# A router between two stages of a one-core transformer kernel: logits, ranks and fillers changed

## What is computed

```
h     = rmsnorm(x, norm2[1])
probs = softmax(h @ router)                 # 8 experts for each of 512 tokens
top_p, top_i = top_k(probs, 2)
top_p = top_p / sum(top_p)
gates = sum(one_hot(top_i, 8) * top_p)      # token x expert
out   = sum over e of gates[:, e] * swiglu(h, w_gate[e], w_up[e], w_down[e])
```

## Time and profile before

| | |
|---|---|
| profiled execution | 2717.13 us |
| its span | 2715.3 us |
| mean granted clock of TensorE | 0.986 |
| TensorE busy | 2601.9 us, 96% |
| VectorE busy | 1575.6 us, 58% |
| ScalarE busy | 1189.9 us, 44% |
| router's stage | from about 1043.5 to 1070.3 us |
| experts' stage | from 1071.4 us |

### The profile page before, as it was taken

How to read it: one execution, slowest core, us unless ns; L and a number is a source line. 1 busy time by engine, 2 the same in 40 slices (tenths; PEclk the granted TensorE clock), 3 DMA queues, 4 the chain that set the end, 5 groups by cost and what they waited for, 6 DMA issues and landing times. The chain is left out here.

```text
span 2715.3 us, 54780 instructions
## 1 busy us (share of the span) xinstructions
PE 2601.9 (96%) x22741; PEld 2088.9 (77%) x22741; DVE 1575.6 (58%) x1974; ACT 1189.9 (44%) x1532; POOL 318.4 (12%) x360
## 2 busy tenths in 40 slices
PE   8999999999999988999999998999899999999998
PEld 7677678888777767788888887864778797788887
DVE  6747454244484755667676676377565545564462
ACT  5644343122355443555656564345334433432232
POOL 5123000000110401011111100021410000000002
PEclk9999899999999999999999999999999999999999
DMA  4200244334220022787787777412023342333341
GB/s 140 82 9 3 63 114 110 86 93 112 71 89 25 4 56 73 274 285 276 282 289 275 279 276 241 123 42 74 6 72 117 93 140 70 86 97 99 91 110 53
DMA packets 351884, 331.12 MB, mean 122 GB/s; under 512 B 17273, under 2 KB 269525, under 8 KB 351605
## 3 DMA queue, kind: packets, MB, share of 16 engines
q1 hardware_dynamic: 348101, 317.76, 37.6%
q0 software_dynamic: 3392, 11.14, 1.1%
q10 hardware_dynamic: 240, 0.07, 0.0%
HBM read 317.41 MB, written 11.53 MB: 121 GB/s over the span
## 5 line engine op out<-in xcount | busy, mean ns | idle before, releaser
L3234 DVE TENSOR_TENSOR experts_w_lo<-experts_raw,experts_w_hi 128x2048 fp32r<-128x2048 f32 (+1 forms) x81 | 167.6, 2079 | 76.2 <-ACT experts_w_hi L3190 74.9
L3234 DVE TENSOR_TENSOR experts_w_lo<-raw_in_act,experts_w_hi 128x2048 fp32r<-128x2048 f32 (+1 forms) x81 | 167.0, 2078 | 58.4 <-ACT experts_w_hi L3190 58.1
L3190 ACT ACTIVATE experts_w_hi<-raw_in_act 128x2048 fp32r<-128x2048 f32 (+1 forms) x81 | 139.7, 1746 | 49.1 <-DMA raw_in_act<-in_moe_up 43.6
L3403 PE MATMUL psum<-experts_w_hi,experts_xg_lo 128*128 128x512 f32 x384 | 155.0, 404 | 5.4 <-DVE experts_w_lo L3234 4.3
L1641 PE MATMUL psum<-keep_act_hi,proj_w_lo 128*128 128x512 f32 x360 | 151.0, 419 | 7.4 <-DVE proj_w_lo L1561 7.4
L3404 PE MATMUL psum<-experts_w_lo,experts_xg_hi 128*128 128x512 f32 x384 | 150.7, 392 | 0.0
L3405 PE MATMUL psum<-experts_w_hi,experts_xg_hi 128*128 128x512 f32 x384 | 150.6, 392 | 0.0
L3190 ACT ACTIVATE experts_w_hi<-experts_raw 128x2048 fp32r<-128x2048 f32 (+1 forms) x81 | 140.4, 1742 | 21.7 <-DMA experts_raw<-in_moe_gate 17.0
L1643 PE MATMUL psum<-keep_act_hi,proj_w_hi 128*128 128x512 f32 x360 | 140.5, 390 | 0.0
L1642 PE MATMUL psum<-keep_act_lo,proj_w_hi 128*128 128x512 f32 x360 | 140.3, 390 | 0.0
L862 PE MATMUL psum<-keep_act_hi,conv_ffn_w_lo 128*128 128x512 f32 x336 | 131.9, 392 | 2.3 <-DVE conv_ffn_hid_lo L913 2.3
(11 more groups left out here) (867 smaller groups left out, 6834.1 us busy)
## 6 DMA issues: line engine op xcount, KB each, us to landing
raw_in_act<-in_moe_gate SPq DMA_DIRECT2D x33, 1024.0 KB, 7.2
experts_raw<-in_moe_up SPq DMA_DIRECT2D x32, 1024.0 KB, 10.4
experts_raw<-in_moe_down SPq DMA_DIRECT2D x32, 768.0 KB, 11.6
raw_in_act<-in_moe_down SPq DMA_DIRECT2D x32, 768.0 KB, 6.8
conv_ffn_raw<-in_w_ffn_in SPq DMA_DIRECT2D x43, 512.0 KB, 5.0
experts_raw<-in_moe_gate SPq DMA_DIRECT2D x17, 1024.0 KB, 8.7
raw_in_act<-in_moe_up SPq DMA_DIRECT2D x16, 1024.0 KB, 5.2
proj_raw<-in_w_in SPq DMA_DIRECT2D x18, 768.0 KB, 4.4
```

The costliest lines, as they stand in the source:

```text
L3190: act.activation(w_hi[v % 2][:, s], raw[ring][:, 0:n], ACT.Copy).then_inc(rounded, 1)
L3234: dve.tensor_tensor(w_lo[v % 2][:, s], raw[ring_of(2 * v + q)][:, 0:n], w_hi[v % 2][:, s].bitcast(F32), ALU.subtract).then_inc(split, 1)
L3403: pe.matmul(out, lhs[1][:, first + k, :], w_hi[slot][:, cols], start=begin and k == 0, stop=False)
```

## The change

The logits are made with plain fp32 products, in token order at once: for each of the eight tiles and each token group, h is the loaded operand and the eight columns of the router's weights are streamed. With that the rounding and the rest of h and of the weights go, as do the copy by expert and its four transposes. Their buffers go too. The logits are compared unscaled, and only the argument of the exponential is multiplied by the root. The root itself is one square root on ScalarE, with its table asked for in advance by a dummy activation, and a reciprocal on VectorE. The sums of squares stand behind the logits and two turns of rows.

The comparisons of all four token groups are one instruction each (256 elements). The prefix sum reads PSUM; chosen is turned twice, and ScalarE copies the second for the later product. The number of tiles is one comparison against four limits and one sum. ScalarE also copies the nth table, which VectorE did. The eight pieces of rows are spread: two before the sums, three behind them, three behind the tile sum, with ScalarE's keeps in groups of 1, 3, 2 and 2. The turns of the identity become 0, 6 and 0 in the router in place of 10, 22 and 24, and 10 in place of 22 at the opening of the experts.

```diff
@@ class Route
     def aside(self, job):
         def scalar(act, j, group):
                     self.square(act, k)
-                    self.round(act, k)
         def vector(dve, j, group):
                     self.weigh(dve, k)
-            if group >= 2:
-                for k in (2 * group - 4, 2 * group - 3):
-                    self.rest(dve, k)
@@ scalar
-            act.wait_ge(m.early.landed, w_landed)
-            act.activation(w_hi[:, :, :], w, ACT.Copy).then_inc(parts, 1)
             for k in LATE:
-                route.round(act, k)
                 route.square(act, k)
+            act.activation(no_root[:, :], m.ones[:, 0:1], ACT.Sqrt)
             act.wait_ge(summed, 1)
-            act.activation(root_tok[:, :], ps[:, 0, 0:TT], ACT.Ln, scale=1.0 / D, bias=m.eps[:, 0:1]).then_inc(root, 1)
-            act.wait_ge(root, 1)
-            act.activation(root_tok[:, :], root_tok[:, :], ACT.Exp, scale=-0.5).then_inc(root, 1)
-            act.wait_ge(root, 2)
+            act.activation(length_tok[:, :], ps[:, 0, 0:TT], ACT.Sqrt, scale=1.0 / D, bias=m.eps[:, 0:1]).then_inc(root, 1)
+            act.wait_ge(v_done, STEPS["root"])
-            keep(range(0, 3))
-            act.wait_ge(centred, 1)
+            keep(range(0, 1))
+            act.wait_ge(centred, 3)
             act.activation(prob[:, :, :], prob[:, :, :], ACT.Exp).then_inc(exped, 1)
-            keep(range(3, 8))
+            keep(range(1, 4))
             act.wait_ge(t_full, 2)
+            act.activation(chosen_t[0:E, :], ps[0:E, 7, :], ACT.Copy).then_inc(chosen_kept, 1)
+            act.wait_ge(t_full, 3)
             act.wait_ge(filled, 5)
             act.activation(tall[PROB, :], ps[0:E, 1, :], ACT.Copy).then_inc(prob_kept, 1)
+            keep(range(4, 6))
+            act.wait_ge(nth_full, 1)
+            act.activation(tall[NTH, :], ps[0:E, 7, :], ACT.Copy).then_inc(nth_kept, 1)
+            keep(range(6, 8))
@@ tensor
-            turn_identity(m, pe, ps[:, 2, 0:P], 10)
-            pe.wait_ge(parts, 2)
+            pe.wait_ge(m.early.landed, w_landed)
             for k in range(DT):
-                ...
-            last.then_inc(full, 1)
+                pe.wait_ge(route.weighted, k + 1)
+                for t in range(TT):
+                    last = pe.matmul(ps[:, 7, t * E:(t + 1) * E], h[:, k, t * P:(t + 1) * P], w[:, k, :], ...)
+            last.then_inc(logits_full, 1)
+            for n in range(2):
+                turn(n)
             (the four products of the sums)
-            (the four transposes of the logits by expert)
-            for n in range(8):
+            for n in range(2, 5):
                 turn(n)
-            turn_identity(m, pe, ps[:, 1, 0:P], 22)
+            pe.wait_ge(root, 1)
+            turn_identity(m, pe, ps[:, 1, 0:P], 6)
             pe.wait_ge(v_done, STEPS["prob"])
-            for b, src in enumerate((chosen, prob)):
+            for b, src in ((0, chosen), (7, chosen), (1, prob)):
                 (four transposes each)
-            pe.wait_ge(v_done, STEPS["chosen_t"])
+            pe.wait_ge(chosen_kept, 1)
             (the product that counts chosen over experts)
             pe.wait_ge(v_done, STEPS["tiles"])
             (the product that sums the tiles)
+            for n in range(5, 8):
+                turn(n)
             pe.wait_ge(prob_kept, 1)
-            turn_identity(m, pe, ps[:, 1, 0:P], 24)
+            pe.wait_ge(nth_kept, 1)
@@ vector
+            step(dve.tensor_copy(logits[:, :, :], ps[:, 7, 0:TT * E].rearrange("p (t e) -> p t e", t=TT)))
+            dve.wait_ge(root, 1)
+            step(dve.reciprocal(root_tok[:, :], length_tok[:, :]))
+            dve.tensor_reduce(top[:, :], logits[:, :, :], AX.X, ALU.max).then_inc(centred, 1)
+            (prob = (logits - top) * root_tok in two instructions)
-            for t in range(TT):
-                (two comparisons of 128 x 64)
+            own = logits[:, :, :].unsqueeze(3).to_broadcast([P, TT, E, E])
+            other = logits[:, :, :].unsqueeze(2).to_broadcast([P, TT, E, E])
+            step(dve.tensor_tensor(above[:, :, :, :], other, own, ALU.is_gt))
+            step(dve.tensor_tensor(ties[:, :, :, :], other, own, ALU.is_equal))
             dve.wait_ge(t_full, 1)
-            step(dve.tensor_copy(chosen_t[0:E, :], ps[0:E, 0, :]))
-            step(dve.tensor_tensor_scan(run[0:E, :], ..., chosen_t[0:E, :], 0.0, ALU.mult, ALU.add))
-            (one step and three pairs of steps for the limits)
+            step(dve.tensor_tensor_scan(run[0:E, :], ..., ps[0:E, 0, :], 0.0, ALU.mult, ALU.add))
+            step(dve.tensor_scalar(more[0:E, :], limits[0:E, :], run[0:E, T - 1:T], None, ALU.is_lt))
+            step(dve.tensor_reduce(tiles[0:E, :], more[0:E, :], AX.X, ALU.add))
+            dve.wait_ge(chosen_kept, 1)
             step(dve.tensor_tensor(tall[RUN, :], run[0:E, :], chosen_t[0:E, :], ALU.mult))
-            dve.wait_ge(nth_full, 1)
-            step(dve.tensor_copy(tall[NTH, :], ps[0:E, 7, :]))
@@ experts_phase, tensor
-            turn_identity(m, pe, ps[:, 7, 0:P], 22)
+            turn_identity(m, pe, ps[:, 7, 0:P], 10)
             list_slots(0)
             turn_identity(m, pe, ps[:, 7, 0:P], 52)
```

More of the change, by code:

```diff
@@ L2720, in __init__ @@
         self.h = m.nc.alloc_sbuf_tensor_at("route_h", [P, DT, T], F32, offset=ROUTE_AT)
[L2721 to L2732, removed]
+        self.ring = m.nc.alloc_sbuf_tensor_at("route_sq", [P, 3, T], F32, offset=ROUTE_AT + DT * T * 4)
+        self.squared, self.added, self.weighted = (m.nc.alloc_semaphore(f"route_{n}") for n in ("squared", "added", "weighted"))
     def square(self, act, k):
@@ L2805, in route_phase @@
         tall, wide = ph.sb("tall", [P, T]), ph.sb("wide", [P, 3, N])
-        tiles, more, begin, end = (ph.sb(n, [P, 1]) for n in ("tiles", "more", "begin", "end"))
+        LIMITS = -(-T // SLOTS)
+        tiles, begin, end = (ph.sb(n, [P, 1]) for n in ("tiles", "begin", "end"))
+        limits, more = (ph.sb(n, [P, LIMITS]) for n in ("limits", "more"))
         mine, shift, before = (ph.sb(n, [P, N]) for n in ("mine", "shift", "before"))
@@ L2810, in route_phase @@
         ps = ph.banks()
[L2811 to L2815, removed]
+        consts, filled, summed, root, logits_full, centred, exped, turned, kept, stored = (
+            ph.sem(n) for n in ("consts", "filled", "summed", "root", "logits_full", "centred", "exped", "turned", "kept", "stored"))
+        v_done, t_full, chosen_kept, prob_kept, nth_full, nth_kept, ended, made = (
+            ph.sem(n) for n in ("v_done", "t_full", "chosen_kept", "prob_kept", "nth_full", "nth_kept", "ended", "made"))
         block = ph.enter_context(nc.Block())
@@ L2819, in route_phase @@
         LATE = range(route.EARLY, DT)
-        LIMITS = range(SLOTS, T, SLOTS)
         STEPS, n = {}, 0
-        for name, steps in (("prob", 11 + 2 + 2 * TT + 8), ("chosen_t", 1), ("tiles", 2 + 2 * len(LIMITS)), ("wide", 11)):
+        for name, steps in (("root", 12 + 2), ("prob", 2 + 4 + 4), ("tiles", 3), ("wide", 10)):
             n += steps
@@ L2886, in turn @@
                 last.then_inc(turned, 1)
[L2888 to L2889 removed]
+            pe.wait_ge(m.early.landed, w_landed)
             for k in range(DT):
[L2891 to L2894, removed]
[L2895 removed]
+                pe.wait_ge(route.weighted, k + 1)
+                for t in range(TT):
+                    last = pe.matmul(ps[:, 7, t * E:(t + 1) * E], h[:, k, t * P:(t + 1) * P], w[:, k, :], start=k == 0 and t == 0,
+                                     stop=k == DT - 1 and t == TT - 1, skip_group_check=True)
+            last.then_inc(logits_full, 1)
+            for n in range(2):
+                turn(n)
             pe.wait_ge(route.added, DT - 1)
@@ L2940, in _ @@
                 route.weigh(dve, k)
-            dve.wait_ge(parts, 1)
-            dve.tensor_tensor(w_lo[:, :, :], w, w_hi[:, :, :].bitcast(F32), ALU.subtract).then_inc(parts, 1)
-            for k in range(route.EARLY - 2, DT):
-                route.rest(dve, k)
             for k in LATE:
                 route.add(dve, k)
-            dve.wait_ge(full, 1)
-            dve.tensor_copy(by_expert[:, :], ps[0:E, 1, :]).then_inc(by_expert_done, 1)
             dve.wait_ge(consts, 5)
```

44 lines of the change are left out of this document (10 added, 34 removed).

## The result

| | before | after |
|---|---|---|
| median (runs), on one chip | 2719.03 us (4) | 2798.84 us (4), 2795.84 to 2803.45 |
| ratio after / before, 95% interval | | 1.0293 [1.0278, 1.0307] |
| profiled execution, its span | 2717.13, 2715.3 us | 2795.84, 2793.6 us |
| granted clock, mean | 0.986 | 0.970 |

The changed kernel is 2.9% slower. I had forecast 2715.2 us and a range up to 2722.6, so the forecast is wrong by ten times what a measurement can tell. The 78.3 us between the two spans, split at four points that both traces have.

The account below looks back on a forecast made before the run. It took TensorE, busy 96%, to be bound where it waits or fills time in the router's stretch. Gains of 3.7 (router) and 0.5 (experts' opening), 4.2 us, off a mean of 2719.4 gave 2715.2 us; range 2709.0 to 2722.6.

Parts of the forecast that it names:

- The step that failed: From the router to the code behind the gather: all of it moves by what the router saves, 4.2 us with the opening.
- five cases: The forecast of 2715.2 us (chance 0.45) and four rivals about router and experts' opening, all inside 0.3% (8.2 us).
- first rival: Router's logits: the clock falls after some 41 of 64 narrow records, net 0.5 us slower than before; chance 0.20.
- Logits and root: Router's head: 64 records take 7.4 us, reciprocal ready at 1053.3 where VectorE began at 1053.35; about nothing gained.
- Ranks: VectorE's comparisons in the router: two of 0.43 us in place of eight, first transpose at 1057.35 not 1058.48, 1.1 gained.
- Scan to placing products: Router after the ranks: scan from PSUM 1.25 us, tiles ready at 1059.75 not 1062.36, placing products from 1062.5 to 1063.7.
- The new last one: Router's end: SyncE's last store, after ScalarE's last kept rows, ends the stage at 1065.8 to 1067.3; 3.7 us gained.
- Opening: Start of the experts: 10 turns, not 22, at the low clock; 5.3 us against 5.8, 0.5 gained.
- Gather: Behind the experts' opening: the 52 turns take 5.87 us inside the gather's 7.4, so they don't show.
- third rival: Experts' opening: the 52 turns run at the low clock, 11.6 us, eating the whole gain, 2719.4 us; chance 0.05.

Follow-up runs that it names:

- pad22: The changed kernel with 22 empty TensorE instructions behind the router's last product: 2719.16 us, ratio 1.0012 to the kernel before.
- before_m44: The kernel before with 30 in place of 52 identity turns behind the first lists, 44 TensorE instructions less: 2794.85 us, ratio 1.0289.
- pad96: The changed kernel with 96 empty TensorE instructions behind the router's last product: 2769.24 us in one run.

## Why the prediction was wrong

**The step that failed** stood at the end of its first part: "what the router saves moves the gather, and everything behind the gather, by the same amount". Everything behind was taken to be the same work at another time. But the change also takes 44 instructions from TensorE's stream, and I costed their number at nothing; the rows that held the warning were the page's queue line (111 packets, none of them inside a loop that runs for 500 us) and the count of 22741. All five cases of the forecast lay within 0.3%, because none was about the code behind the router. This step is 75.6 of the 78.3 us; pad22 and before_m44 show it in both directions. In its place the runs showed a loop that was loaded anew in every pass, nine packets each, with TensorE held 5.5 to 6.2 us at the branch and up to 2.3 us more at the next block's border.

**The first rival's mechanism came true**, and was given 0.20. It was right (the clock falls while only eight columns per record stream) and its size was too small: I let it fall after 41 of 64 records, it fell after 24. By the router's own steps, all counted from the last w_out product:

- *Logits and root*: reciprocal ready 16.7 us in (1061.04), where VectorE's chain had begun at 11.1. I had them equal; 5.6 lost. A record at the full clock took 0.11 as costed (24 in 2.7 us).
- *Ranks*: from there to the end of the probabilities 3.9 us against 5.1. I had 1.1 gained; 1.1 measured, the two comparisons at 0.42 each.
- *Scan to placing products*: 5.5 us against 9.3: 3.8 gained. The scan from PSUM took 1.21, as it did from SBUF; taken 1.25.
- *The new last one*: as written. VectorE's last step ended at 1072.6, the next stage began at 1074.95, 3.7 us after ScalarE's last kept rows (1071.26). From placing products to that stage 4.5 us against 3.7.
- These sum to 1.4 lost up to the next stage, where I had 3.7 gained.
- *Opening*: 5.44 us against 5.80; 0.4 gained, 0.5 taken.
- *Gather*: the 52 turns took 8.65 us, not 5.87, the clock being 0.50 until 1086.1, and outlasted the rows: 1.1 lost. This is the third rival (given 0.05), in a quarter of its size.

With the loop at a fast place, the changed router so costs about 2 us over the old one, which pad22's 1.0012 [0.9999, 1.0025] can't tell from nothing: with the place costed I would have been right about the 0.3% and wrong about the side. VectorE's and ScalarE's steps gave what I had put down for them and more (1.1 at the ranks, 3.8 from scan to placing); it was the plain products, at the low clock, that took it back.

## What to carry to other kernels

When a change adds or removes instructions ahead of a long loop, count them on the loop's engine: 44 fewer out of 16,368 cost 2.9% here, and 22 empty ones gave it back. Look for the instruction queue inside the loop's window before believing any wait there, and check that the engine named as a releaser ended when the wait did. And give narrow products their price at the low clock as well: here 24 wide ones, with their copy and turns, took 7.5 us where 64 narrow ones took 11.3 for the same logits.

## What the hardware did that I had not expected

- A loop of 1720 TensorE instructions ran seven passes without one instruction packet, or with nine packets and 6.8 to 13.6 us more in each, by its place alone. The passes are longest (85 us, loop at 16,340) where a block ends three instructions behind the loop's start, and the shortest with packets (78.5, at 16,444) are those where the next border is 155 on.
- TensorE's branch to the loop's start took 0.21 to 0.24 us where nothing was loaded and 5.4 to 6.6 us where its target was.
- A loop that was being reloaded can stop being so (pad96, from its seventh pass on).
- A PSUM operand cost the scan nothing (1.21 us either way).
